# One denoising step on one core: the scan's additions reordered, a gathered group norm, seven-product output projections, and filter features moved into the input projection

## What is computed

```python
def _rwkv_mix(rw, lp, s0f, s0b):
    ...
    g = jax.nn.sigmoid(gd) @ lp['g_up']
    ...
        bonus = jnp.sum(hd(r) * hd(kd) * lp['r_k'], axis=-1, keepdims=True) * hd(v)
        outs.append(yd + bonus.astype(jnp.float32))
    ...
    y = outs[0] + outs[1]
    mu = jnp.mean(y, axis=-1, keepdims=True)
    var = jnp.mean(jnp.square(y - mu), axis=-1, keepdims=True)
    y = ((y - mu) * lax.rsqrt(var + GN_EPS)).reshape(B, L, W).astype(rw.dtype)
    y = (y * lp['ln_g'] + lp['ln_b']) * g
...
    out = jnp.concatenate([o, r_out], axis=-1) @ lp['w_out']
...
    hdn = jnp.sin(fr[0] * (z @ lp['f_w0'].astype(f32) + lp['f_b0'].astype(f32)))
    ...
    z = _short_conv(h @ lp['w_in'] + lp['b_in'], lp['conv_w'], lp['conv_b'])
    ...
    return u @ lp['w_out'] + lp['b_out']
```

## Time and profile before

| quantity | value |
|---|---|
| timed runs | 5159.09, 5168.80, 5169.05 us; median 5168.8 |
| profiled execution | 5160.96 us |
| its span | 5159.2 us |
| mean granted clock of TensorE | 0.937 of full |
| PE, DVE, ACT, POOL busy | 88%, 49%, 20%, 8% of the span |

### The profile page before, as it was taken

The page is one execution under the profiler, slowest core; times in us unless marked ns, Lnnn a source line. Parts: engine busy times, 40 slices in busy tenths (PEclk is TensorE's granted clock), DMA queues, the critical chain, the costliest instruction groups (busy, mean ns, idle before and its releaser), DMA issues. The chain is left out here.

```text
span 5159.2 us, 73362 instructions
## 1 busy us (share of the span) xinstructions
PE 4524.0 (88%) x30480; PEld 3509.3 (68%) x30480; DVE 2522.4 (49%) x3679; ACT 1017.9 (20%) x1892; POOL 394.1 (8%) x385
## 2 busy tenths in 40 slices
PE   5989789954799949899999989969997889999997
PEld 3656378843788835677777767747776457777775
DVE  6755367777688851422223333447776242222332
ACT  2000056652344410200000022221121020000002
POOL 0000100000000000121110011100000011211000
PEclk7999989976899979999999999979998999999998
DMA  4354100010000001111114212220010311111520
GB/s 148 122 202 146 50 15 7 5 69 1 5 0 0 0 32 40 71 39 41 41 56 125 60 68 85 79 102 31 16 37 28 113 63 41 41 41 33 145 71 37
DMA packets 253992, 297.55 MB, mean 58 GB/s; under 512 B 18306, under 2 KB 209131, under 8 KB 252686
## 3 DMA queue, kind: packets, MB, share of 16 engines
q1 hardware_dynamic: 243486, 250.40, 15.0%
q10 hardware_dynamic: 7648, 30.81, 1.5%
q0 software_dynamic: 2704, 14.16, 0.8%
HBM read 240.68 MB, written 51.51 MB: 57 GB/s over the span
## 5 line engine op out<-in xcount | busy, mean ns | idle before, releaser
L896 PE MATMUL acc<-arena 128*128 128x288 f32 x4928 | 1205.5, 408 | 38.1 <-ACT arena L336 24.2
L896 PEld LDWEIGHTS acc<-arena 128*128 128x128 f32 x4928 | 941.6, 191 | 302.4 <-issue 38.3
L443 PE MATMUL acc<-arena 128*128 128x384 f32 x1824 | 606.5, 495 | 65.9 <-DMA arena<-in_ab_w_out 25.8
L702 PE MATMUL acc<-arena 128*128 128x288 f32 x2464 | 597.8, 406 | 0.0
L443 PEld LDWEIGHTS acc<-arena 128*128 128x128 f32 x1824 | 351.1, 194 | 309.3 <-issue 78.9
L702 PEld LDWEIGHTS acc<-arena 128*128 128x128 f32 x2464 | 468.2, 190 | 129.4
L2192 PE MATMUL acc<-arena 128*128 128x288 f32 x1344 | 333.2, 412 | 16.3 <-ACT arena L336 11.7
L2192 PEld LDWEIGHTS acc<-arena 128*128 128x128 f32 x1344 | 259.1, 193 | 90.6 <-issue 16.8
L2544 PE MATMUL acc<-arena 128*128 128x256 f32 x1280 | 280.9, 380 | 5.2 <-DVE arena L2716 3.4
L2544 PEld LDWEIGHTS acc<-arena 128*128 128x128 f32 x1280 | 241.9, 190 | 40.6 <-DVE arena L2716 6.2
L1332 DVE TENSOR_REDUCE arena<-acc 128x1 f32<-128x1280 f32 (+1 forms) x144 | 195.5, 1358 | 101.7 <-PE acc L1258 94.4
(11 more groups left out here) (345 smaller groups left out, 5908.9 us busy)
## 6 DMA issues: line engine op xcount, KB each, us to landing
arena<-in_ffn_w SPq DMA_DIRECT2D x44, 1024.0 KB, 5.3
arena<-in_ffn_w SPq DMA_DIRECT2D x64, 704.0 KB, 6.5
arena<-in_ada_w SPq DMA_DIRECT2D x20, 2048.0 KB, 10.3
scratch_x_d<-arena SPq DMA_DIRECT2D x3, 4608.0 KB, 17.2
scratch_z_d<-arena SPq DMA_DIRECT2D x24, 576.0 KB, 2.8
arena<-scratch_z_d SPq DMA_DIRECT2D x12, 1152.0 KB, 6.4
arena<-in_hy_w_in SPq DMA_DIRECT2D x12, 1024.0 KB, 5.1
arena<-in_ab_w_in SPq DMA_DIRECT2D x22, 512.0 KB, 4.2
```

The lines of the kernel that those rows point to most:

```text
L443: last = pe.matmul(k.bank(tc, TC), slab[j][:, kt, :], src(kt)[:, tc * TC:(tc + 1) * TC], start=(kt == 0), stop=(kt == n_k - 1))
L702: mm = pe.matmul(acc(m, j)[:, s, :], slot[left[m][j]][:, kt, :], right[m][:, kt, s * TS:(s + 1) * TS], start=(kt == 0), stop=(kt == KH - 1))
L896: last = pe.matmul(acc(w, m)[:, s, :], left[:, kt, :], right[:, kt, s * TS:(s + 1) * TS], start=(kt == 0), stop=(kt == 3))
```

## The change

The scan's bonus additions come behind the Gram masks, the first half of `ark1` comes ahead of the output's additions, and the copies of the decays get a function of their own (`decay_ends`). In `stage_rwkv_post` the variances of all heads are gathered: PE sums each head's squares into its own row of one 72 x 128 tile (row 8c + 2t + head for block c of 128 tokens), one root and one reciprocal do for all, and PE spreads the rows back with a matrix that POOL makes (`spread_head_rows`). ACT keeps the gates. SP asks for the mixer's first weights and for the residual in this stage. A new `stage_projection` does both output projections in seven products, in 4 pairs of tiles. For the mixer its loads are already under way; for the convolution (`loaded=False`) SP and ACT issue the loads of the sources, and POOL those of the residual once the sources are in. The features' layers become jobs F0 and F1 of `stage_hyena_in`, behind the products of pairs 1 to 3; its buffers move, and POOL's first weight sums wait for the norm. `stage_filter_features` is removed. The diff, cut to its core (`head_window` picks 72 columns of a constant that is one where the head is):

```diff
-                dve.drain()
+            def decay_ends():
...
-                for d in range(2):
-                    dve.drain()
-                    dve.tensor_tensor(ya[:, :, cols(i, d)], ya[:, :, cols(i, d)], tmp[:, 4 * d:4 * d + 4, :], ALU.add)
...
+                for d in range(2):
+                    dve.tensor_tensor(ya[:, :, cols(i, d)], ya[:, :, cols(i, d)], tmp[:, 4 * d:4 * d + 4, :], ALU.add)
+                    dve.drain()
...
+                if ahead:
+                    ark1(i, 1)
...
-                    ark1(i, 1).then_inc(dve_s.sem, 1)
+                    dve.drain()
+                    decay_ends().then_inc(dve_s.sem, 1)
...
+def head_window(k, t, c):
...
+    o, w = CCOL["heads"]
+    at = CST + o + 70 - (8 * c + 2 * t)
+    return k.arena[:, at:at + 72]
...
+def spread_head_rows(k, pool, rows, made):
+    pool.tensor_copy(rows.rearrange("p (n o) -> p n o", o=64),
+                     k.ident[0:72, 0:72].rearrange("p (n o) -> p n o", o=1).broadcast_to([72, 72, 64])).then_inc(made, 1)
...
+            for p in range(2):
+                sp.dma_start(slab[p], wview[:, :, 256 * p:256 * p + 256]).then_inc(slab_in[p], 16)
+            for m in range(KT):
+                load_x_tile(k, sp, scratch, m, x_in)
...
+            def variances(t):
+                pe.wait_ge(squared, t + 1)
+                for c in range(9):
+                    last = pe.matmul(k.bank(6)[0:72, 0:128], head_window(k, t, c), sq[:, t, c * 128:(c + 1) * 128],
+                                     start=(t == 0 and c == 0), stop=(t == 3 and c == 8))
...
-                pe.wait_ge(squared, t + 1)
                 if t:
-                    pe.wait_ge(done, t)
-                for tc in range(3):
-                    last = pe.matmul(k.bank(3 + tc, TC), k.const("blockones"), sq[:, t % 2, tc * TC:(tc + 1) * TC], start=True, stop=True)
-                last.then_inc(var_ready, 1)
-                pe.wait_ge(rooted, t + 1)
+                    pe.wait_ge(gate_kept, t)
...
+                last.then_inc(gated, 1)
+                if t:
+                    variances(t - 1)
+            variances(3)
+            pe.wait_ge(inverted, 1)
+            pe.wait_ge(rows_made, 1)
+            for t in range(4):
+                if t == 0:
+                    pe.wait_ge(centred, 4)
+                if t == 1:
+                    pe.wait_ge(gate_kept, 4)
+                if t >= 2:
+                    pe.wait_ge(normed, t - 1)
+                for c in range(9):
+                    last = pe.matmul(k.psum[:, 1536 * (t % 2) + c * 128:1536 * (t % 2) + (c + 1) * 128], rows[:, 64 * (8 * c + 2 * t):64 * (8 * c + 2 * t) + 128], rstd, start=True, stop=True)
+                last.then_inc(spread, 1)
...
+            def keep_gate(t):
+                act.wait_ge(gated, t + 1)
+                for tc in range(3):
+                    last = act.activation(out[:, t, tc * TC:(tc + 1) * TC], k.bank(3 + tc, TC), ACT.Copy)
+                last.then_inc(gate_kept, 1)
...
-                act.wait_ge(var_ready, t + 1)
-                for tc in range(3):
-                    last = act.activation(root[:, t % 2, tc * TC:(tc + 1) * TC], k.bank(3 + tc, TC), ACT.Sqrt, bias=eps, scale=1.0 / C)
-                last.then_inc(rooted, 1)
+                act.activation(sq[:, t, :], ya[:, t, :], ACT.Square).then_inc(squared, 1)
+            act.wait_ge(var_ready, 4)
+            act.activation(rstd, k.bank(6)[0:72, 0:128], ACT.Sqrt, bias=eps[0:72, :], scale=1.0 / C).then_inc(rooted, 1)
+            for t in range(4):
...
-                dve.wait_ge(rooted, t + 1)
-                dve.reciprocal(root[:, t % 2, :], root[:, t % 2, :])
+            dve.wait_ge(rooted, 1)
+            dve.reciprocal(rstd, rstd).then_inc(inverted, 1)
+            for t in range(4):
+                dve.wait_ge(spread, t + 1)
+                dve.tensor_tensor(ya[:, t, :], k.psum[:, 1536 * (t % 2):1536 * (t % 2) + T], ya[:, t, :], ALU.mult).then_inc(normed, 1)
+                if t:
+                    dve.wait_ge(scaled, t)
+                    dve.tensor_tensor(out[:, t - 1, :], out[:, t - 1, :], ya[:, t - 1, :], ALU.mult)
+            dve.wait_ge(scaled, 4)
+            dve.tensor_tensor(out[:, 3, :], out[:, 3, :], ya[:, 3, :], ALU.mult)
...
+def stage_projection(k, tag, src, layer, scratch, weights, loaded, bias=None, src_rows=None):
...
+    ORDER = ("M1", "M2", "M6", "M5", "M7", "M3", "M4")
...
+            if not loaded:
+                load(0)
+                for m in range(4, KT):
+                    sp.dma_start(src[:, m, :], src_rows(m)).then_inc(src_in[1], 16)
+                load(1)
+            for p in range(2, pairs):
+                sp.wait_ge(prod, prod_at(p - 2, "M4"))
+                load(p)
...
+            if not loaded:
+                pool.wait_ge(src_in[0], 64)
+                pool.wait_ge(src_in[1], 64)
+                for m in range(KT):
+                    load_x_tile(k, pool, scratch, m, x_in)
+            for p in range(pairs):
+                a11, a12, a21, a22, s1, s2, s3, s4 = parts(p)
+                pool.wait_ge(slab_in[p % 2], 16 * (p // 2 + 1))
...
+                pool.tensor_tensor(s1, a21, a22, ALU.add).then_inc(step_done, 1)
+                pool.tensor_tensor(s3, a11, a21, ALU.subtract)
+                pool.wait_ge(step_done, step_at(p, 1))
+                pool.tensor_tensor(s2, s1, a11, ALU.subtract).then_inc(step_done, 1)
+                pool.wait_ge(step_done, step_at(p, 2))
+                pool.tensor_tensor(s4, a12, s2, ALU.subtract).then_inc(wsum_ready, 1)
...
+                pe.wait_ge(slab_in[p % 2], 16 * (p // 2 + 1))
+                if p == 0 and not loaded:
+                    pe.wait_ge(src_in[0], 64)
+                product(p, "M1", a11, h11)
+                if p == 0 and not loaded:
+                    pe.wait_ge(src_in[1], 64)
+                product(p, "M2", a12, h21)
+                pe.wait_ge(wsum_ready, p + 1)
+                if p == 0:
+                    pe.wait_ge(sums_ready, 2)
+                product(p, "M6", s2, t2)
...
+            if not loaded:
+                for m in range(4):
+                    act.dma_start(src[:, m, :], src_rows(m)).then_inc(src_in[0], 16)
...
+            if not loaded:
+                dve.wait_ge(src_in[0], 64)
+            tt(t1, h12, h11, ALU.subtract).then_inc(sums_ready, 1)
+            dve.wait_ge(sums_ready, 1)
+            if not loaded:
+                dve.wait_ge(src_in[1], 64)
+            tt(t2, h22, t1, ALU.subtract).then_inc(sums_ready, 1)
...
-    heads = k.tiles(OA0, 8, T)
-    stage_gemm(k, "mix", lambda kt: heads[:, kt, :], KT, A["ab_w_out"][0].rearrange("(k p) n -> p k n", p=128),
-               KT, H0, evac_residual(k, 0, 0), x_from=scratch["x_d"])
...
+    stage_projection(k, "mix", k.tiles(OA0, 8, T), 0, scratch, weights, True)
...
+    jobs = [(p, m) for p in range(pairs) for m in ORDER + (("F0", "F1") if 1 <= p < 4 else ())]
...
+            sp.wait_ge(x_gone, 16)
+            sp.wait_ge(norm.scaled, 3 * KT)
+            sp.dma_start(feat[0:33, :], consts["feat"]).then_inc(fw_in, 16)
...
+                sp.dma_start(w3[64 * o:64 * o + 64, :, :, :], A["hy_f_w3"][0].rearrange("p (o d n) -> p o d n", o=2, d=2)).then_inc(w3_in, 16)
...
+                if p == 8:
+                    sp.wait_ge(hx_set, 1)
+                    sp.wait_ge(ws_set, 4)
+                    sp.dma_start(k.at(FT0, 5120), consts["dft"]).then_inc(tab_in, 16)
+                    sp.dma_start(k.at(IT0, 4096), consts["idft"]).then_inc(tab_in, 16)
+            sp.wait_ge(prod, prod_at(pairs - 1, "M1"))
+            sp.dma_start(k.at(PT0, 512), consts["pdft"]).then_inc(tab_in, 16)
...
-                if p == 1:
-                    pool.wait_ge(x_gone, 16)
+                if p == 0:
                     pool.wait_ge(norm.scaled, 3 * KT)
...
+                if 2 <= p < 6:
...
+                    pool.tensor_tensor(ws[rows, o, :], w3[rows, o, 0, :], w3[rows, o, 1, :], ALU.subtract if d else ALU.add).then_inc(ws_set, 1)
...
+                if job(p, m) >= 4:
+                    p0, m0 = jobs[job(p, m) - 4]
+                    if m0 == "M1":
+                        pe.wait_ge(copied, p0 + 1)
+                    elif m0 in ("F0", "F1"):
+                        pe.wait_ge(scaled_sum, 2 * (p0 - 1) + (2 if m0 == "F1" else 1))
+                    else:
+                        pe.wait_ge(added, added_at(p0, m0))
...
+                if 1 <= p < 4:
+                    n = p - 1
+                    if n:
+                        pe.wait_ge(sined, n)
+                    else:
+                        pe.wait_ge(fw_in, 160)
+                    src = hd[low, :] if n else feat[0:33, :]
+                    for f in range(2):
+                        claim(p, f"F{f}")
+                        for q in range(2):
```

(17 more changed lines are left out.)

## The result

The changed kernel takes **5028.0 us** in the median of four runs (5022.9 to 5043.9), where the kernel before takes 5166.7 beside it: a ratio of 0.974, with a 95% interval of 0.9723 to 0.9757. Forecast were 5031 us and a range of 5006 to 5060. The profiled execution has a span of 5024.4 us, 134.8 less than before. This is its busy line, which answers to the earlier trace rows: PE works 24 us less, and idles 110 us less.

What follows compares the result with a forecast made beforehand. PE, working 88% of the span, bounds the kernel, so only less PE work or idling pays. Terms 15 + 40 + 25 + 43 + 10 = 133 took 5161 to 5028, plus 3 for a low profiled run: 5031 us, range 5006 to 5060.

Steps and rivals of the forecast that it cites:

- Scan: In the scan, moving two bonus additions behind the Gram masks starts level 1 earlier: 15 us, bounds 0 and 24.
- 0.9 per chunk: In the scan, level 1 starts at 1785.7 instead of 1786.62, saving 0.9 us in each of 16 chunks computing ahead.
- the two last chunks ... gain nothing: In the scan, the two last chunks have no LoRA products in between, so their gain is zero.
- Stage after the scan: After the scan, gathered variances with one small reciprocal end at 44 instead of 83.9: 40 us, bounds 36 and 42.
- Rival (a): PE's clock stays low in the new stage after the scan, costing about 18 us: 5049 us; chance 0.12.
- Mixer: Mixer's output projection in seven products, its initial wait gone: 118.2 instead of 143.0, 25 us, bounds 21 and 29.
- weights and residual are there: At the mixer projection's start, the 25.8 us wait goes because its loads ran during the stage after the scan.
- Features: The 50.1 us filter-feature stage hides in the convolution's input projection: 43 us gained, bounds 36 and 44.
- Rival (b): Features do not hide in the input projection: late sine or tables put half of 43 us back, 5053; chance 0.08.
- Output projection: Convolution's output projection in seven products, POOL's loads delaying its sums: 136.0 instead of 145.8, 10 us, bounds 17 and 4.
- Rival (c): Scan keeps its full 1.5 us per chunk (+9), projections' weight sums do not block (+4, +7): 5011; chance 0.08.
- Rival (d): Both seven-product output projections run at the low clock, 218 us more: 5249, slower than before; chance 0.02.

Runs made afterwards that it cites:

- the version with all edits: Changed kernel with bonus additions behind level 0's first copies, spare matmuls before the spreading, DVE/POOL sums in turn, POOL's first sums earlier in both convolution projections: 5015.9 us.
- a form of the kernel before: Kernel before, with ACT waiting for both first weight slabs before asking for the mixer projection's residual: that stage took 131.8 us instead of 142.9.

## Why the prediction was right, and where only its sum was

- **Scan** (15, measured 15.8): the mechanism was right, and the run with `ark1` put back confirms that only the additions count. That the sum came out is in part luck, as its terms were off against each other: 0.9 per chunk should have been 1.35, mostly because the price of 1.50 for the additions was that beside POOL's copies; of the 16 chunks that were to gain, the context's first and the first latent one lost 0.1 and 0.25; and "the two last chunks ... gain nothing" should have read that they lose, since nothing covers the additions there (0.3 us, and 2.5 in the last).
- **Stage after the scan** (40, measured 42.8, just above the upper bound of 42): right step by step, each a little shorter, and the reciprocal is the larger part (28.0). Rival (a), the low clock in this stage, was not refuted but came in part: see below. Its argument that each burst after a pause began at the low level read the rows too broadly: in the stage before, groups of six rows behind 2.84 to 10.17 us of idle time took 3.59 to 4.21 us, but those behind 1.61 us took 2.20.
- **Mixer** (25, measured 27.7): the total was right. The wait goes as forecast, but the reason given, that "weights and residual are there", credits the lead with too much: all but 4.0 of the stage's 15.3 us until the first product were the slabs' transfer beside the residual's and go as soon as the slab is asked for first (11.2 us of the stage); the lead adds 4.1. POOL's and DVE's turns let M6 start at 11.6 and not 13.5, and the restart at the low clock (1 us) did not come: the 416 rows from M6 on take 0.243 each.
- **Features** (43, measured 40.5): hidden as forecast. Three groups of matmuls cost 2.15 us each, 6.5 (5.8 forecast), POOL's wait for the norm 1.0 (1.1). Of the other 2.1, 1.7 are the norm's first sums, 17.44 us for 48 rows at a granted clock of 0.90, where before it was 15.75 at 1.00. The forecast put that at nothing. It is no chance of this execution: both profiles of the kernel before have 15.75, and the eleven others 17.3 to 17.4, the one with the features apart among them. What brings it stays open, as in FFN 0. Rival (b) falls: no product waits for a sine. Rows of PE from the end of the second pair on:

```profile
3022.58 2.15 PE L2497 MATMUL acc<-arena 33*64 33x288 f32 x8
...
3024.66 27.43 PE L2468 MATMUL acc<-arena 128*128 128x288 f32 x112
...
3052.02 2.15 PE L2497 MATMUL acc<-arena 64*64 64x288 f32 x8
```

- **Output projection** (10, measured 9.9, and 11.8 in the eight other profiles): right by its own steps, to M6 within 0.2 us. That the total is met to 0.1 is luck. What it named as in the way, POOL's loads ahead of its sums, was the cause, and the run without it gains 9.5 to 11.4 us.
- **Rival (c)** came in part: a chunk gained 1.35 of its 1.5 us, while the weight sums did block, for 1.71 and 7.80 us. **Rival (d)** falls: the 896 rows of both projections take 224.5 us by the page, 0.25 a row.

## What to carry to other kernels

Before crediting a load issued ahead, look at what its transfer runs beside: here the order of two loads was worth 11.2 us and, on top of it, a whole stage of lead 4.1. An engine that issues DMAs and also computes for the bound engine should compute first, if its inputs come first (9.5 us). And when work is moved behind a cover, check the last round of the loop, which may have none.

## What the runs showed that was not expected

**The same pause costs nothing in one execution and 6 us in another.** In the stage after the scan PE idles 1.44 us before the spreading. In six of eight profiles of this form the spreading then takes 8.3 us (granted clock 1.00 in the changed kernel's); in two it takes 14.6 and 14.8 (0.55 and 0.54), as here:

```profile
1850.62 14.56 PE L2083 MATMUL acc<-arena 72*128 72x128 f32 x72 [1.44 <-DVE arena L2115]
```

That is rival (a), in a quarter of these profiles and in one group of rows. The pause of 1.84 us in the scan's last chunk goes either way too. With the spare matmuls in the pause the spreading took 8.20 us in both profiles, which is too few to show that they help.

**Most of the spread between executions lies in one place that the change does not touch.** The windows of 640 to 770 us (the beginning of attention), of the changed kernel and of the version with all edits:

```profile
640.00:770.00 130.00, 110.79 (x747) 89.38 (x746) 91.79 (x124) 70.27 (x141) 11.17 (x16) 0.88 0.06 15
```

```profile
640.00:770.00 130.00, 111.77 (x650) 89.38 (x649) 80.74 (x113) 61.75 (x127) 10.02 (x15) 0.76 0.06 15
```

With the same busy time PE gets through 747 rows at a granted clock of 0.88, and 650 at 0.76. Over all 13 profiles the two go together: those with 0.87 or 0.88 there reached the scan at 1225.4 to 1231.4 us, the three with 0.82 to 0.84 at 1233.7 to 1235.2, and the three with 0.72 to 0.76, one of them a form of the kernel before, at 1243.7 to 1247.5. What decides it stays open. A version should therefore be judged by its stages as well as by its total.

**DVE and POOL pay for each other on both sides.** Alone, DVE's column sum takes 2.56 us and POOL's weight sum 1.09 to 1.27; side by side they take 3.3 to 3.7 each, about the sum of the two. The Trainium skill, page "SBUF — State Buffer", section "Who interferes with whom", has them exclude each other for a whole instruction, and the run that keeps them apart agrees with it.
